# Where operand tiles stand modulo 256 bytes: moved low weights and activation tiles in a float32 two-block transformer kernel

## The chip, the core and the metric

The kernel runs on one NeuronCore of a Trainium2 chip. The metric is the device time of one execution in microseconds (us). TensorE does matrix products from SBUF into PSUM; VectorE, ScalarE and GpSimd do the rest; 16 DMA engines bring data from HBM. SBUF has 128 partitions, and an address in this text is a byte offset within a partition.

## What is computed

Two transformer blocks of width 2048 on 256 tokens, batch 1, all in float32. Both blocks are norm, projection, attention, projection, residual, norm, gated MLP (5632 wide), residual; the second has 16 more tokens in front (272 in all) and a convolution over three positions in its gate branch. Cut to the products with large weights:

```python
# first block                                       # weights
h = rms_norm(x, g) * (1 + scale_a) + shift_a
proj = h @ w_in                                     # 2048 x 5456
mixed = concat([diff_out, dsa_out]) @ w_o           # 2048 x 2048
h = rms_norm(x, g) * (1 + scale_f) + shift_f
ff = (silu(h @ w_gate) * (h @ w_up)) @ w_down       # 2048 x 5632 (twice), 5632 x 2048
# second block: w_in_2 2048 x 3904, w_q_up, w_kv_up, w_out_2, and
gc = conv_b + sum(conv_w[i] * shifted(h @ w_gate_2, i))
y = (silu(gc) * (h @ w_up_2)) @ w_down_2
```

`mod = silu(c) @ w_ada + b_ada` (2048 x 12288) gives shifts, scales and gates of the first block.

## The kernel before, in words

Activations are kept transposed: tile k of `x_hi` and `x_lo` holds features 128k to 128k + 127 on the partitions and the tokens along the free side. A float32 product is made from three faster ones (type float32r). Each operand is split into a high part (rounded to that type) and a low part (what is left), and the kernel adds high x high, low x high and high x low. The three are lines 2115, 2116 and 2117 in `dense` (line 2077). The stationary operand is a 128 x 128 piece of a weight buffer, the moving operand an activation tile of 256, 258 or 272 columns.

Weights come in units of 4 x 128 rows by 512 columns (1 MB, four buffers `raw`), in one order for the whole program. For each unit ScalarE writes `w_hi` (line 932) and VectorE `w_lo = raw - w_hi` (line 1462). There are two slots of each, `w_hi0`, `w_hi1`, `w_lo0`, `w_lo1` of 8192 bytes, used in turn. TensorE then does 4 output blocks (m) x 4 tiles (k) x 3 = 48 matmuls on the unit. A product over 2048 features has four units (`K16`), over 5632 features twelve (`K44`, the last four with three tiles).

In order of time: first projection (44 units, part by part: all columns for tiles 0 to 3, then for 4 to 7, and so on; 4 of the 44 have three output blocks), attention, `out1` with `w_o`, gate and up of the first block (11 pairs of `mlp1`), down (`hid_hi`, `hid_lo` as moving tiles), then the second block: its projection with 272 columns, two latent projections (272 columns, 8 short calls), `out2` with 258 columns, gate with 258 and up with 256 columns, and `down2` (lines 2796 to 2798), which has the hidden tiles as the stationary operand and 512 columns of weights as the moving one.

The places are made by `place` (line 236), which puts one tensor behind the other from byte 2208 on, rounded up to 32. `raw`, `w_hi` and `w_lo` have 8192 bytes each, `x_res`, `x_hi` and `x_lo` are 16 tiles of 272 float32 (17408 bytes = 68 x 256; one tile 1088 = 4 x 256 + 64), `hid_hi` and `hid_lo` 44 tiles of 256 float32 (45056 = 176 x 256; one tile 1024). Two gaps of 64 bytes stand between `x_hi` and `x_lo` and between `hid_hi` and `hid_lo`. So, counted from byte 2208 and modulo 256, all weight buffers are at 0, tile k of `x_hi` at 64k, of `x_lo` at 64k + 64, all tiles of `hid_hi` at 64, of `hid_lo` at 128.

Of the kernel before, what the change touches and what calls it, by code (L numbers as in the profile page):

```python
# [22 lines left out]
F32R = mybir.dt.float32r  # L23
# [4 lines left out]
P = 128  # L28
D = 2048
KT = D // P  # L30
S = 256
# [5 lines left out]
COLS = 512  # L37
UK = 4
RAW = 4
SPLIT = 2  # L40
# [115 lines left out]
def in1_width(n):  # L156

    return PROJ1 - 10 * COLS if ORDER_IN1[n] == 10 else COLS
# [69 lines left out]
def program(nc, a):  # L228
    with ExitStack() as ctx:
# [1 line left out]
            return ctx.enter_context(nc.semaphore(name))  # L231


        cursor = [2208]

        def place(name, shape, dt=F32, at=None):
            size = 4 * int(np.prod(shape[1:]))
            if at is None:
                at, cursor[0] = cursor[0], (cursor[0] + size + 31) // 32 * 32
            return nc.alloc_sbuf_tensor_at(name, shape, dt, offset=at)  # L240
# [8 lines left out]

        raw = [place(f"raw{i}", [P, UK * COLS]) for i in range(RAW)]  # L250
        w_hi = [place(f"w_hi{i}", [P, UK * COLS], F32R) for i in range(SPLIT)]
        w_lo = [place(f"w_lo{i}", [P, UK * COLS], F32R) for i in range(SPLIT)]
        x_res = place("x_res", [P, KT, N2])
        x_hi_at = cursor[0]
        x_hi = place("x_hi", [P, KT, N2], F32R)
        cursor[0] += 64
        x_lo_at = cursor[0]
        x_lo = place("x_lo", [P, KT, N2], F32R)
        branch_f = place("branch_f", [P, KT, S], at=x_hi_at)
        xmeta = place("xmeta", [META, D], at=x_lo_at)  # L260
        arena = cursor[0]
        hid_hi = place("hid_hi", [P, FT, S], F32R)
        cursor[0] += 64
        hid_lo = place("hid_lo", [P, FT, S], F32R)
        arena_end = cursor[0]
        cst = place("cst", [P, C_WIDTH])
# [11 lines left out]
        gain = place("gain", [P, 2, KT])  # L278
# [141 lines left out]
        norms, at = {}, dict(sq=0, col=0, presum=0, norm=0, group=0, use=0, split=0)  # L420
# [21 lines left out]
        def one(rows=P):  # L442
# [8 lines left out]
        kpe = proj2[0:64, T2_KPE, :]  # L451
        kpg = proj2[0:64, T2_CQ, :]
        norm("attn_pre", S, D, [[x_res[:, t, 0:S] for t in range(KT)]],
             [(0, x_res[:, t, 0:S], gain[:, 0, t:t + 1], x_hi[:, t, 0:S], x_lo[:, t, 0:S],
               mod[:, SH_A + t:SH_A + t + 1]) for t in range(KT)], True, given=x_sum)
        norm("diff", S, P, [[dout[:, h, :]] for h in range(8)],
             [(h, dout[:, h, :], lamv[:, 7:8], x_hi[:, h, 0:S], x_lo[:, h, 0:S], None) for h in range(8)], True)
# [1 line left out]
             [(0, branch_a[:, t, :], gain[:, 1, t:t + 1], branch_a[:, t, :]) for t in range(KT)], False,  # L459
             branch_a_ssq, direct=4)  # L460
        norm("ffn_pre", S, D, [[x_res[:, t, 0:S] for t in range(KT)]],
             [(0, x_res[:, t, 0:S], gain[:, 0, t:t + 1], x_hi[:, t, 0:S], x_lo[:, t, 0:S],
               mod[:, SH_F + t:SH_F + t + 1]) for t in range(KT)], True, column=True)
        norm("ffn_post", S, D, [[branch_f[:, t, :] for t in range(KT)]],
             [(0, branch_f[:, t, :], gain[:, 1, t:t + 1], branch_f[:, t, :]) for t in range(KT)], False,
# [122 lines left out]
        K16 = [(4 * q, 4) for q in range(4)]  # L588
        K_O = K16[2:] + K16[:2]
        K44 = [(4 * q, 4) for q in range(8)] + [(32 + 3 * q, 3) for q in range(4)]  # L590
        FOUR = [P] * 4
# [1484 lines left out]
        def _(pe):  # L2076
# [11 lines left out]
            def dense(units, rows, hi, lo, n, cols=None, width=COLS, step=1, last_unit=True, base=0, ready=None,  # L2088
# [38 lines left out]
                else:  # L2127
                    t.at += 4

            def xs(n):  # L2130
                return (lambda k: x_hi[:, k, 0:n]), (lambda k: x_lo[:, k, 0:n])

# [196 lines left out]
            for u in range(44):  # L2329
                part, n = divmod(u, 11)  # L2330
                if u == 0:
                    pe.wait_ge(tile_done, 4)
                    pe.wait_ge(bank_freed, 4)
                if n == 0 and part:
                    pe.wait_ge(n_lo, norms["attn_pre"]["first"]["split"] + 4 * part + 4)
                if n in (0, 2, 4, 6):
                    ada_quarter(ADA_IN1 + 2 * part, n // 2)
                ur.at = in1_unit(part, n)
                dense([K16[part]], TAIL1 if in1_width(n) < COLS else FOUR, *xs(S), S, width=in1_width(n),
                      banks=lambda m: in1_bank(u, m), lag=IN1_BANKS,  # L2340
                      tile_ready=None if u else "attn_pre")
                if n == 6:
                    ada_columns(ADA_IN1 + 2 * part)
                if n == 7:
                    s = ADA_IN1 + 2 * part + 1
                    pe.wait_ge(beside_used, 4 * part + 4)
                    pe.wait_ge(ada_copied, s)
                    for j in range(4):
                        ins = pe.matmul(bank[7][:, j:j + 1], acc_beside[:, P * j:P * j + P], one(), start=True,
                                        stop=True)  # L2350
                    ins.then_inc(ada_cols, 1)
                if part == 3 and n in (5, 7, 8, 10):
                    rotate_rows({5: 0, 7: 1, 8: 2, 10: 3}[n])
                if u == 23:
                    pe.wait_ge(vec_in, 16 * VEC_LOADS)
                    for j in range(3):
                        ins = pe.transpose(bank[6][:, P * j:P * j + P], packs[:, 1 + j, :], ident)
                    ins.then_inc(packs_turned, 1)
# [235 lines left out]
            spread("ffn_pre")  # L2594

            def mlp1(i, tile_ready=None, ada_block=None):
                dense(K16, FOUR, *xs(S), S, tile_ready=tile_ready,
                      step=2 if ada_block is not None else (lambda j: 9 if j == 0 else 1) if tile_ready else 1)
                if ada_block is not None:
                    pe.wait_ge(up_freed, up.value(4))  # L2600
                    ada_sum(ada_block, bank[7])
                dense(K16, FOUR, *xs(S), S, base=4, bank7=None if ada_block is None else ada_block + 1)
            mlp1(0, "ffn_pre")
            loop(4, (8, 4, 12, 4), lambda i: mlp1(i + 1, ada_block=i + ADA_MLP1))
            loop(6, (8, 4, 8, 4), lambda i: mlp1(i + 5))
# [227 lines left out]
```

## Time and profile before

| | |
|---|---|
| median of 3 runs | 2582.85 us (2581.18 to 2584.17) |
| profiled execution, its own time | 2583.03 us |
| its span in the trace | 2581.2 us |
| TensorE busy | 2475.4 us, 96% |
| VectorE, ScalarE, GpSimd busy | 1439.2, 1032.2, 292.0 us |
| mean granted clock of TensorE | 0.979 |
| read from HBM | 498.04 MB, 194 GB/s over the span |

The trace has every instruction's start and duration. Matmuls are pipelined: one that starts while another still runs is normal, and the pace is the time from one start to the next. The granted clock is 1.00 where TensorE runs at 2.4 GHz and 0.50 where it runs at 1.2 GHz.

### The profile page before, as it was taken

The numbers are of one execution on the slowest core, as the hardware profiler recorded it, in microseconds if no ns is written. First come the engines' busy times: TensorE is split into PE (matmuls) and PEld (weight loads), VectorE is DVE, ScalarE is ACT, GpSimd is POOL, SyncE is SP. The second block draws the span as 40 slices with busy tenths as digits, with TensorE's granted clock in tenths as the row PEclk, the third lists the DMA queues.
The fourth block names the chain that finished last, engine by engine and source line by source line (L and its number), as shares of the span: only waits on it lengthen the run. The fifth ranks groups of instructions, "written<-read, shape, count | busy, mean of one in ns | idle before, by whom it ended". The sixth has DMA issues, their size and how long they took to land.

```text
span 2581.2 us, 45664 instructions
## 1 busy us (share of the span) xinstructions
PE 2475.4 (96%) x18966; PEld 2296.1 (89%) x18966; DVE 1439.2 (56%) x1918; ACT 1032.2 (40%) x1332; POOL 292.0 (11%) x372
## 2 busy tenths in 40 slices
PE   6999988989999999999989998999999999999999
PEld 4999847979999999999979997778899999998877
DVE  3687657966674444444455555655655555554443
ACT  3533244344434343333334335443444444443332
POOL 5000122410100000011113002103000000000000
PEclk8999989989999999999989999999999999999999
DMA  9887864977786555555554451324455555554553
GB/s 353 290 288 268 286 211 168 337 271 237 249 294 200 184 185 189 178 185 186 179 146 149 139 160 54 126 71 131 132 188 185 179 179 179 180 185 169 193 202 131
DMA packets 263858, 504.18 MB, mean 195 GB/s; under 512 B 17152, under 2 KB 26283, under 8 KB 263467
## 3 DMA queue, kind: packets, MB, share of 16 engines
q1 hardware_dynamic: 257899, 494.97, 57.3%
q10 hardware_dynamic: 5840, 7.52, 0.9%
q8 instruction: 87, 1.43, 0.2%
q14 instruction: 32, 0.26, 0.0%
HBM read 498.04 MB, written 2.10 MB: 194 GB/s over the span
## 4 chain that ended last, share of the span: by engine, by line
PE 78%; DVE 8%; ACT 4%; issue 4%; DMA 3%; SPq 1%; ACTq 1%; POOL 1%; DVEq 0%; POOLq 0%
PE bank L2115 21%; PE bank L2117 20%; PE bank L2116 20%; ACT w_hi L932 3%; DVE w_lo L1462 3%; PE bank L2798 3%; PE bank L2796 3%; PE bank L2797 3%; PE bank L2150 1%; DMA raw<-in_w_in 1%; DVE ada_acc L1490 1%; DVE tmp L1596 1%; SPq L643 1%; PE bank L2259 1%; DMA staged<-in_w_ada 1%
## 5 line engine op out<-in xcount | busy, mean ns | idle before, releaser
L1462 DVE TENSOR_TENSOR w_lo<-raw,w_hi 128x2048 fp32r<-128x2048 f32 (+3 forms) x386 | 862.7, 2235 | 937.6 <-ACT w_hi L932 937.3
L2115 PE MATMUL bank<-x_hi,w_hi 128*128 128x256 f32 (+2 forms) x4608 | 1316.6, 286 | 37.1 <-DVE w_lo L1462 20.3
L2117 PE MATMUL bank<-x_hi,w_lo 128*128 128x256 f32 (+2 forms) x4608 | 1306.4, 283 | 0.0
L2116 PE MATMUL bank<-x_lo,w_hi 128*128 128x256 f32 (+2 forms) x4608 | 1300.7, 282 | 0.0
L932 ACT ACTIVATE w_hi<-raw 128x2048 fp32r<-128x2048 f32 (+3 forms) x386 | 718.7, 1862 | 1027.7 <-PE bank L2117 745.3
L2115 PEld LDWEIGHTS bank<-x_hi,w_hi 128*128 128x128 f32 x4608 | 872.2, 189 | 74.7 <-issue 41.3
L2116 PEld LDWEIGHTS bank<-x_lo,w_hi 128*128 128x128 f32 x4608 | 872.0, 189 | 1.2 <-issue 1.2
L2117 PEld LDWEIGHTS bank<-x_hi,w_lo 128*128 128x128 f32 x4608 | 871.8, 189 | 0.0
L2117 PE MATMUL bank<-hid_hi,w_lo 128*128 128x256 f32 x704 | 198.5, 282 | 0.0
L2115 PE MATMUL bank<-hid_hi,w_hi 128*128 128x256 f32 x704 | 196.8, 280 | 0.9 <-DVE w_lo L1462 0.9
L2116 PE MATMUL bank<-hid_lo,w_hi 128*128 128x256 f32 x704 | 197.1, 280 | 0.0
L797 POOL TENSOR_TENSOR hid_lo<-gpad,hid_hi 128x256 f32 x88 | 61.0, 726 | 996.4 <-ACT hid_hi L1417 503.2
L2796 PE MATMUL bank<-w_hi,hid_hi 128*128 128x512 f32 x352 | 138.4, 393 | 2.1 <-DVE gpad L2057 1.4
L2798 PE MATMUL bank<-w_lo,hid_hi 128*128 128x512 f32 x352 | 140.0, 398 | 0.0
L2797 PE MATMUL bank<-w_hi,hid_lo 128*128 128x512 f32 x352 | 138.0, 392 | 0.0
L2115 PEld LDWEIGHTS bank<-hid_hi,w_hi 128*128 128x128 f32 x704 | 133.7, 190 | 1.5 <-issue 1.5
L2116 PEld LDWEIGHTS bank<-hid_lo,w_hi 128*128 128x128 f32 x704 | 132.2, 188 | 0.0
L2117 PEld LDWEIGHTS bank<-hid_hi,w_lo 128*128 128x128 f32 x704 | 131.7, 187 | 0.0
L1490 DVE SCALAR_TENSOR_TENSOR ada_acc<-raw,csilu,ada_acc 128x512 f32<-128x512 f32 x120 | 97.2, 810 | 3.8 <-DMA raw<-in_w_ada 0.4
L2796 PEld LDWEIGHTS bank<-w_hi,hid_hi 128*128 128x128 f32 x352 | 66.2, 188 | 17.7 <-DVE w_lo L1462 2.0
L2797 PEld LDWEIGHTS bank<-w_hi,hid_lo 128*128 128x128 f32 x352 | 66.2, 188 | 16.2
L2798 PEld LDWEIGHTS bank<-w_lo,hid_hi 128*128 128x128 f32 x352 | 66.1, 188 | 14.3
(337 smaller groups left out, 1662.0 us busy)
## 6 DMA issues: line engine op xcount, KB each, us to landing
raw<-in_w_gate SPq DMA_DIRECT2D x88, 1024.0 KB, 5.2
raw<-in_w_up SPq DMA_DIRECT2D x88, 1024.0 KB, 5.2
raw<-in_w_ada SPq DMA_DIRECT2D x72, 1024.0 KB, 6.5
raw<-in_w_in SPq DMA_DIRECT2D x68, 1024.0 KB, 5.5
raw<-in_w_down SPq DMA_DIRECT2D x64, 1024.0 KB, 5.0
raw<-in_w_down SPq DMA_DIRECT2D x32, 768.0 KB, 4.3
beside<-in_w_ada SPq DMA_DIRECT2D x16, 1024.0 KB, 7.7
raw<-in_w_o SPq DMA_DIRECT2D x16, 1024.0 KB, 6.5
```

The lines of the kernel that those rows point to most:

```text
L643: sp.dma_start(staged[4 * s + q][:, :].rearrange("p (k c) -> p k c", k=nk), src).then_inc(staged_in[4 * s + q], 16)
L797: pool.tensor_tensor(lo, gpad[:, m, 0:S], hi, ALU.subtract).then_inc(hid_low, 1)
L932: act.activation(w_hi[ps][:, 0:width], raw[slot][:, 0:width], ACT.Copy).then_inc(hi_ready, 1)
L1462: dve.tensor_tensor(w_lo[ps][:, 0:width], raw[slot][:, 0:width], w_hi[ps][:, 0:width], ALU.subtract).then_inc(raw_free[slot], 1)
L1490: ins = dve.scalar_tensor_tensor(ada_acc[:, :], w, s, ada_acc[:, :], ALU.mult, ALU.add)
L1596: dve.scalar_tensor_tensor(dst, src, gcol, spread_row(name, g, rows, n["n"]), ALU.mult, ALU.mult).then_inc(n_app, 1)
L2115: pe.matmul(out, wh[:, k, c], hi(k0 + k), start=a0, stop=False)
L2116: pe.matmul(out, wh[:, k, c], lo(k0 + k), start=False, stop=False)
L2117: ins = pe.matmul(out, wl_[:, k, c], hi(k0 + k), start=False, stop=z)
L2796: pe.matmul(out, hi, wh[:, k, :], start=j == 0 and k == 0, stop=False)
L2797: pe.matmul(out, lo, wh[:, k, :], start=False, stop=False)
L2798: ins = pe.matmul(out, hi, wl_[:, k, :], start=False, stop=j == 11 and k == nk - 1)
```

## The change

It moves operands in SBUF and changes nothing else: no instruction, wait, transfer or order.

- `w_lo1` is put first, then 128 bytes are left free, then `w_lo0`, then 96 bytes. So `w_lo0` stands at 128, `w_lo1` at 0, and what follows starts at 224.
- The two gaps of 64 bytes go. `x_hi`, `x_lo` then start at 224 both (tile k at 224 + 64k), `hid_hi` and `hid_lo` at 224.
- A new function `spaced` lays tiles of 256 columns over the room of `x_hi` and `x_lo`, 1024 bytes apart with 256 bytes more after each four, so that the tiles of one unit of weights have one place: `xin` for the first projection at 48, 80, 96, 112 for the four units (high and low alike), `xff` for gate and up of the first block at 192 (high) and 192, 192, 224, 224 (low). The norms ahead of these stages write there, and `dense` reads there.
- `out1` and the second block go on using `x_hi` and `x_lo`.

```diff
-        cursor = [2208]
+        first = 2208
+        cursor = [first]
...
-        w_lo = [place(f"w_lo{i}", [P, UK * COLS], F32R) for i in range(SPLIT)]
+        w_lo1 = place("w_lo1", [P, UK * COLS], F32R)
+        cursor[0] += 128
+        w_lo = [place("w_lo0", [P, UK * COLS], F32R), w_lo1]
+        cursor[0] += 96
         x_res = place("x_res", [P, KT, N2])
         x_hi_at = cursor[0]
         x_hi = place("x_hi", [P, KT, N2], F32R)
-        cursor[0] += 64
         x_lo_at = cursor[0]
         x_lo = place("x_lo", [P, KT, N2], F32R)
+
+        def spaced(name, phases):
+
+            tiles = []
+            for part, start in enumerate((x_hi_at, x_lo_at)):
+                tiles.append([])
+                for k in range(KT):
+                    at_ = 4 * S * k + 256 * (k // 4) + (phases[k // 4][part] - (start - first)) % 256
+                    room = place(f"{name}{part}_{k}", [P, S + 8], F32R, at=start + at_ // 32 * 32)
+                    tiles[part].append(room[:, at_ % 32 // 4:at_ % 32 // 4 + S])
+            return tiles
+        xin_hi, xin_lo = spaced("xin", [(48, 48), (80, 80), (96, 96), (112, 112)])
+        xff_hi, xff_lo = spaced("xff", [(192, 192), (192, 192), (192, 224), (192, 224)])
...
         hid_hi = place("hid_hi", [P, FT, S], F32R)
-        cursor[0] += 64
         hid_lo = place("hid_lo", [P, FT, S], F32R)
...
-             [(0, x_res[:, t, 0:S], gain[:, 0, t:t + 1], x_hi[:, t, 0:S], x_lo[:, t, 0:S],
+             [(0, x_res[:, t, 0:S], gain[:, 0, t:t + 1], xin_hi[t], xin_lo[t],
...
-             [(0, x_res[:, t, 0:S], gain[:, 0, t:t + 1], x_hi[:, t, 0:S], x_lo[:, t, 0:S],
+             [(0, x_res[:, t, 0:S], gain[:, 0, t:t + 1], xff_hi[t], xff_lo[t],
...
-                dense([K16[part]], TAIL1 if in1_width(n) < COLS else FOUR, *xs(S), S, width=in1_width(n),
+                dense([K16[part]], TAIL1 if in1_width(n) < COLS else FOUR, *tiles(xin_hi, xin_lo), S, width=in1_width(n),
...
-                dense(K16, FOUR, *xs(S), S, tile_ready=tile_ready,
+                dense(K16, FOUR, *tiles(xff_hi, xff_lo), S, tile_ready=tile_ready,
...
-                dense(K16, FOUR, *xs(S), S, base=4, bank7=None if ada_block is None else ada_block + 1)
+                dense(K16, FOUR, *tiles(xff_hi, xff_lo), S, base=4, bank7=None if ada_block is None else ada_block + 1)
```

## Rows read from the trace of the kernel before

**Rows 1.** The page: busy time, chain that ended last, the two split instructions.
```profile
PE 2475.4 (96%) x18966; PEld 2296.1 (89%) x18966; DVE 1439.2 (56%) x1918; ACT 1032.2 (40%) x1332; POOL 292.0 (11%) x372
...
PE 78%; DVE 8%; ACT 4%; issue 4%; DMA 3%; SPq 1%; ACTq 1%; POOL 1%; DVEq 0%; POOLq 0%
...
L1462 DVE TENSOR_TENSOR w_lo<-raw,w_hi 128x2048 fp32r<-128x2048 f32 (+3 forms) x386 | 862.7, 2235 | 937.6 <-ACT w_hi L932 937.3
...
L932 ACT ACTIVATE w_hi<-raw 128x2048 fp32r<-128x2048 f32 (+3 forms) x386 | 718.7, 1862 | 1027.7 <-PE bank L2117 745.3
```

**Rows 2.** Stages: window, its us, busy us (instructions) by engine, granted clock, DMA share, GB/s.
```profile
43.00:323.00 280.00, 274.94 (x2258) 257.72 (x2259) 203.42 (x278) 107.32 (x119) 26.55 (x25) 0.99 0.82 287
...
556.00:1067.50 511.50, 504.65 (x4256) 500.42 (x4257) 278.32 (x225) 206.47 (x194) 29.50 (x41) 1.00 0.64 212
1067.50:1319.50 252.00, 251.09 (x2133) 250.35 (x2133) 103.20 (x51) 92.62 (x73) 29.53 (x29) 1.00 0.51 172
1342.00:1556.00 214.00, 211.03 (x1612) 197.17 (x1612) 122.81 (x165) 85.75 (x109) 22.73 (x23) 0.99 0.51 161
...
1812.00:2329.00 517.00, 509.99 (x4226) 505.51 (x4227) 288.56 (x338) 222.57 (x281) 27.16 (x42) 1.00 0.56 178
2331.00:2577.00 246.00, 245.30 (x1076) 198.81 (x1075) 103.29 (x54) 85.20 (x54) 0.00 (x0) 1.00 0.51 173
```

**Rows 3.** TensorE in order of time (start, us): first and 193rd, gate and up.
```profile
999.84 0.28 PE L2115 MATMUL bank<-x_hi,w_hi 128*128 128x256 f32 x1
...
1022.24 0.28 PE L2115 MATMUL bank<-x_hi,w_hi 128*128 128x256 f32 x1
```

**Rows 4.** In order of time: first and 193rd, last up block of the first block.
```profile
1044.95 0.28 PE L2115 MATMUL bank<-x_hi,w_hi 128*128 128x256 f32 x1
...
1067.57 0.28 PE L2115 MATMUL bank<-hid_hi,w_hi 128*128 128x256 f32 x1
```

**Rows 5.** In order of time: first and 190th, down projection of the first block.
```profile
1195.88 0.28 PE L2115 MATMUL bank<-hid_hi,w_hi 128*128 128x256 f32 x1
...
1218.14 0.28 PE L2115 MATMUL bank<-hid_hi,w_hi 128*128 128x256 f32 x1
```

**Rows 6.** In order of time: first and 37th, first projection.
```profile
235.95 0.28 PE L2115 MATMUL bank<-x_hi,w_hi 128*128 128x256 f32 x1
...
240.15 0.28 PE L2115 MATMUL bank<-x_hi,w_hi 128*128 128x256 f32 x1
```

**Rows 7.** In order of time: second block, 132 matmuls of gate, then 192 of up.
```profile
2195.81 0.28 PE L2115 MATMUL bank<-x_hi,w_hi 128*128 128x258 f32 x1
...
2211.65 0.28 PE L2115 MATMUL bank<-x_hi,w_hi 128*128 128x256 f32 x1
...
2234.26 0.28 PE L2115 MATMUL bank<-x_hi,w_hi 128*128 128x258 f32 x1
```

**Rows 8.** In order of time: 272 columns, 47 matmuls; then 11 with 64 weight columns.
```profile
1441.61 0.29 PE L2115 MATMUL bank<-x_hi,w_hi 128*128 128x272 f32 x1
...
1447.49 0.28 PE L2117 MATMUL bank<-x_hi,w_lo 128*128 128x272 f32 x1
...
1488.47 0.29 PE L2115 MATMUL bank<-x_hi,w_hi 128*64 128x272 f32 x1
...
1489.84 0.28 PE L2117 MATMUL bank<-x_hi,w_lo 128*64 128x272 f32 x1
```

**Rows 9.** 272 columns at the lower clock: first and tenth; their stretch as in rows 2.
```profile
1600.94 0.43 PE L2115 MATMUL bank<-x_hi,w_hi 128*64 128x272 f32 x1
...
1602.98 0.43 PE L2115 MATMUL bank<-x_hi,w_hi 128*64 128x272 f32 x1
...
1600.72:1602.98 2.26, 2.26 (x12) 2.24 (x11) 0.47 (x1) 2.26 (x5) 0.00 (x0) 0.52 0.00 0
```

**Rows 10.** In order of time: first and 115th, second down projection, 512 columns.
```profile
2427.64 0.39 PE L2796 MATMUL bank<-w_hi,hid_hi 128*128 128x512 f32 x1
...
2453.99 0.39 PE L2796 MATMUL bank<-w_hi,hid_hi 128*128 128x512 f32 x1
```

More of the change, by code:

```diff
@@ L2128, in dense, with tiles @@
                     t.at += 4
+            def tiles(hi, lo):
+                return (lambda k: hi[k]), (lambda k: lo[k])
             def xs(n):
```

## The prediction

> **What bounds the kernel now.** I read the page of the profile first, then the busy time by stage, then single matmuls in order of time. TensorE is busy for 2475.4 us of a span of 2581.2 us, and it carries 78% of the chain that ended last [rows 1]. The stages show where: in the gate and up projections of the first block it is busy 504.65 of 511.50 us, in the first down projection 251.09 of 252.00, in the first projection 274.94 of 280.00, and the second block looks alike [rows 2]. So in all dense stages the end is set by how fast TensorE starts one matmul after the other, and nearly every nanosecond per matmul is a nanosecond of the kernel.
>
> The busy time of a matmul (0.28 us) says nothing on that, since matmuls overlap; the reader has to take starts. In the gate and up stage 192 matmuls of 128x256 start between 999.84 and 1022.24 us: 22.40 / 192 = 116.7 ns each, and no wait lies between [rows 3]. The granted clock there is 1.00, the upper level of 2.4 GHz [rows 2], at which 256 columns take 106.7 ns. So each matmul costs 10.0 ns more than its columns. That this is not a fixed price of an instruction is shown by the one place where the same stream runs at the lower level: from 1600.94 to 1602.98 us, at a granted clock of 0.52 over the window, nine matmuls of 272 columns take 2.04 us, 226.7 ns each, which is 272 columns at 1.2 GHz with nothing on top [rows 9]; at the upper level 47 matmuls of 272 columns take 5.88 us, 125.1 ns each, 11.8 ns over their columns [rows 8]. Something is short only at full speed, and the operands' reads are the candidate that this change touches.
>
> **What the trace says of addresses.** Take all places from the first tile, modulo 256 bytes, as the diff does. Now every weight buffer stands at 0, and rows of weights are multiples of 512 bytes. The tiles x_hi and x_lo are 1088 bytes long, so tile k stands at 64k, its low part at 64k + 64: four different pairs in turn. The hidden tiles are 1024 bytes long, so all stand at 64 (high) and 128 (low). Three findings:
> 1. Every steady pace is a multiple of 6.67 ns for the shortest repeat. I call three matmuls (high x high, low x high, high x low, one k) a triple. Down: 189 matmuls in 22.26 us, 353.3 ns a triple = 53 x 6.67 [rows 5]. Gate and up: 350.0 a triple, and the repeat is four triples, 1400 = 210 x 6.67 [rows 3]. With 258 columns: 132 matmuls in 15.84 us, 360.0 = 54 x 6.67 [rows 7]. With 512 columns: 114 in 26.35 us, 693.4 = 104 x 6.67 [rows 10]. This is an estimate of mine from these rows; it says that a tile arrangement that repeats at each triple can gain or lose only in steps of about 6.7 ns.
> 2. The same lines, the same form and the same addresses have two paces. The last up block of the first block starts 192 matmuls in 22.62 us, 117.8 ns each [rows 4], against 116.7 before [rows 3], and the up block of the second block 192 in 22.61 us [rows 7]. The pace also hangs on how the stream was entered. The difference is 3.3 ns a triple.
> 3. With half the weight columns (64) the pace of 272 columns is 1.37 us / 11 = 124.5 ns against 125.1 [rows 8]. So the weights' own reads carry little of the 10 ns, and moving w_lo alone should do little.
>
> **The change, part by part.** No instruction is added or taken away and no wait moves; only addresses. (a) w_lo of slot 0 goes to 128, of slot 1 stays at 0. (b) First projection: tiles now 1024 bytes apart, high and low both at 48, 80, 96, 112 for the four parts. (c) Gate and up of the first block: 192 for both, low at 224 from tile 8. (d) Down: both at 224. (e) Not named in the title, but done: the two gaps of 64 bytes go, so in out1 and in all of the second block x_hi and x_lo stand at the same 224 + 64k, and the second down's stationary tiles at 224.
>
> The counts follow from the loops: first projection 688 triples, gate and up 22 x 64 = 1408, down 4 x 4 x 44 = 704, together 2800. Untargeted: out1 256, second block 2256 (gate and up 1408, in2 496, out2 256, the two latent projections 96), second down 352, together 2864.
>
> Prices. Down repeats at each triple before and after, so it can only step; it is the slowest arrangement of 256 columns that the trace has. I take one step down, 353.3 to 346.7: 704 x 6.67 = 4.7 us. Gate and up come from 350.0, and within one unit of weights all tiles will now have one pair of places, so it too repeats at each triple and must go to 346.7 or up to 353.3. I take 346.7, 3.33 x 1408 = 4.7 us. The first projection has 36 matmuls in 4.20 us, 350.0 a triple [rows 6], so by the same step 3.33 x 688 = 2.3 us. Why down and not up: the room above the columns' time is 10.0 ns a matmul, 30 a triple, so there are about four steps below and the nearest arrangement with constant places (down) is the one that stands highest. For the untargeted 2864 triples no row has equal places for high and low, so I bound them by the spread that one arrangement shows, 3.33 ns a triple to either side [rows 3, 4], plus or minus 9.5 us, and take zero, since no row speaks for a side. (a) is taken at zero by finding 3, within the same bound.
>
> Sum: 4.7 + 4.7 + 2.3 = 11.7 us. The profiled execution took 2583.0 us (span 2581.2), the median of three is 2582.85, so 2583.0 - 11.7 = 2571.3.
>
> **Cover.** A unit of weights is 48 matmuls, 5.60 us. ScalarE's 1.86 and VectorE's 2.24 us for it [rows 1] make 4.1 us, and with 5.55 us per unit that stays hidden; only where VectorE also empties banks is some of it lost, well under 1 us in all. Next late would be the transfers in the first projection: 287 GB/s at a DMA share of 0.82, against 0.64 in gate and up [rows 2]. If the first projection were held by these, its 2.3 us are lost.
>
> **Rules against the trace.** The trace has one form with paces of 116.7 and 117.8 ns and a constant-place arrangement at 117.8 [rows 3 to 5]. The Trainium skill (SBUF — State Buffer, Who interferes with whom) says that TensorE has two independent read ports, one for the moving operand and one for weights, and never waits for anyone; by it places in memory cost nothing and the change gives 0. It also gives (TensorE: Matmul & The Clock Gate, "Wait — 56ns, not 53.3ns?") columns at 2.4 GHz plus about 2.5 ns from start to start, which is 109.2 ns for 256 columns; the trace has 116.7, so it does not agree for these operands. If the whole difference of 7.5 ns went in the 8400 targeted matmuls the time would be 2520, and I don't hold that for likely.
>
> **The rivals.**
> *Second step.* The places were apt enough for two steps, 340.0 ns a triple. Another 2800 x 6.67 = 18.7 us: 2552.6. For it: the 30 ns of room. Against it: all the arrangements of 256 columns in the rows lie within 3.3 ns a triple of each other.
> *Nothing.* The 10 ns are a fixed toll at full speed, and places only shuffle it among neighbours: 2583. For it: weights of 64 and 128 columns hardly differ, and four pairs of places and one pair come within 1% of each other. Against it: the constant-place stage is the slower one in every unit. The skill's rule of independent ports, above, is the same case.
> *Equal places collide.* High and low tile at the same place is new, and it holds in the first projection, in half of gate and up, in down and in all untargeted triples: 688 + 704 + 704 + 2864 = 4960. At the price of the slower pace, 3.33 ns a triple, that is 16.5 us: 2599.5. Set against the targeted gain it decides from about 3500 triples on (11.7 us / 3.33). For it: now the low tile always stands 64 behind the high one, and nothing shows what 0 does. Against it: the high and the low tile are never moving at the same time, they follow each other, and in down a high tile already follows a high one at the same place.
>
> **Numbers.** Forecast (one step in the targeted stages) 0.43, second step 0.15, nothing 0.17, equal places collide 0.25. Faster by over 0.2% (5.2 us, about what a measurement of this kernel can tell from no change) is the first two, 0.58; within it 0.17; slower 0.25. The sides are of both signs, so the forecast's own range, from the bound of the untargeted triples, is 2562 to 2581; the whole range goes from below the second step, 2545, to the collision's price, 2600.
>
> **What would show it.** In the changed kernel's trace: down at 115.6 ns from start to start (three matmuls in 346.7) and gate and up at the same pace for all k in a unit; 113.3 for the second step; 117.8 for none. In the second block, matmuls of 258 columns at 120.0, of 272 at 125, three of 512 at 693, if it is untouched; 116.7 to 118 instead of 117.8 for its 256 columns. I am wrong if the targeted stages keep their pace, if their pace is no multiple of 6.67 a triple, or if the second block's pace moves by more than 1.1 ns a matmul: it has more triples than the targeted part and could outweigh it.

## The result and the profile after

The changed kernel takes 2586.57 us (median of 18), the kernel before in the same runs 2581.53 us: a ratio of 1.0017, 95% interval 1.001 to 1.0024. It is slower by 5 us. One of the 18 executions took 8412.31 us; the ratio leaves it out, and the median of the other 17 is 2586.50. The profiled execution took 2591.96 us, 5 us over the median, so the times below that rest on one trace are paces, which do not depend on how long single waits are.

The page of the changed kernel: against [rows 1] TensorE's busy time has grown by 10.7 us, and that of the other engines has moved by 1.2 us at most.

```profile
span 2590.2 us, 45664 instructions
...
PE 2486.1 (96%) x18966; PEld 2304.7 (89%) x18966; DVE 1439.3 (56%) x1918; ACT 1033.4 (40%) x1332; POOL 291.2 (11%) x372
...
PE 78%; DVE 8%; ACT 5%; issue 4%; DMA 3%; SPq 1%; ACTq 1%; POOL 1%; DVEq 0%; POOLq 0%
...
L1477 DVE TENSOR_TENSOR w_lo<-raw,w_hi 128x2048 fp32r<-128x2048 f32 (+3 forms) x386 | 863.1, 2236 | 942.1 <-ACT w_hi L947 941.8
L947 ACT ACTIVATE w_hi<-raw 128x2048 fp32r<-128x2048 f32 (+3 forms) x386 | 719.3, 1864 | 1029.0 <-PE bank L2132 757.8
```

Single matmuls of the changed kernel in order of time (start, us), gate and up of the first block. The first pair encloses 84 matmuls with both tiles at 192, the second 36 with 192 and 224 and w_lo at 128 (slot 0), the third 36 with 192 and 224 and w_lo at 0 (slot 1):

```profile
1006.73 0.28 PE L2130 MATMUL bank<-xff,w_hi 128*128 128x256 f32 x1
1016.25 0.28 PE L2130 MATMUL bank<-xff,w_hi 128*128 128x256 f32 x1
...
1017.66 0.28 PE L2130 MATMUL bank<-xff,w_hi 128*128 128x256 f32 x1
1021.90 0.28 PE L2130 MATMUL bank<-xff,w_hi 128*128 128x256 f32 x1
...
1023.32 0.28 PE L2130 MATMUL bank<-xff,w_hi 128*128 128x256 f32 x1
1027.60 0.28 PE L2130 MATMUL bank<-xff,w_hi 128*128 128x256 f32 x1
```

9.52 / 84 = 113.3 ns, 4.24 / 36 = 117.8, 4.28 / 36 = 118.9; per triple (three matmuls of one k) 340.0, 353.3 and 356.7. Before, this stage ran at 350.0 [rows 3] or 353.3 [rows 4]. Half of the stage has come to the 340.0 that the prediction called the second step; the other half has lost.

Down (288 matmuls, answers to [rows 5]), the first projection's third part at 96 (24, to [rows 6]), and in the second block up (192) and gate (96, to [rows 7]) and the second down (177, to [rows 10]):

```profile
1148.30 0.28 PE L2130 MATMUL bank<-hid_hi,w_hi 128*128 128x256 f32 x1
1182.38 0.28 PE L2130 MATMUL bank<-hid_hi,w_hi 128*128 128x256 f32 x1
...
188.22 0.28 PE L2130 MATMUL bank<-xin,w_hi 128*128 128x256 f32 x1
191.10 0.28 PE L2130 MATMUL bank<-xin,w_hi 128*128 128x256 f32 x1
...
2079.31 0.29 PE L2130 MATMUL bank<-x_hi,w_hi 128*128 128x256 f32 x1
2102.05 0.28 PE L2130 MATMUL bank<-x_hi,w_hi 128*128 128x258 f32 x1
2114.20 0.29 PE L2130 MATMUL bank<-x_hi,w_hi 128*128 128x258 f32 x1
2125.78 0.29 PE L2130 MATMUL bank<-x_hi,w_hi 128*128 128x256 f32 x1
...
2407.16 0.40 PE L2815 MATMUL bank<-w_hi,hid_hi 128*128 128x512 f32 x1
2448.29 0.39 PE L2815 MATMUL bank<-w_hi,hid_hi 128*128 128x512 f32 x1
```

A triple is 34.08 / 96 = 355.0 in down (353.3 before), 2.88 / 8 = 360.0 at 96 (350.0), 22.74 / 64 = 355.3 in up (353.3), 11.58 / 32 = 361.9 in gate (360.0), 41.13 / 59 = 697.1 in the second down (693.4). Everything but the tiles at 192 is slower.

For whole stages I take the mean over all starts of a stage that follow each other at less than 160 ns (512 columns: 280 ns), which leaves out the waits, times three. Times the triples of the stage this is what the pace is worth:

| stage (triples) | ns a triple before | after | us | forecast us |
|---|---|---|---|---|
| first projection (688) | 352.0 | 355.4 | +2.4 | -2.3 |
| gate and up, first block (1408) | 350.7 | 348.6 | -2.9 | -4.7 |
| down, first block (704) | 353.3 | 354.9 | +1.1 | -4.7 |
| out1 (256) | 351.1 | 355.7 | +1.2 | 0 |
| second block to out2 (848) | 370.8 | 371.4 | +0.5 | 0 |
| gate, second block (704) | 360.1 | 361.3 | +0.8 | 0 |
| up, second block (704) | 353.3 | 355.3 | +1.5 | 0 |
| second down (352) | 693.4 | 698.4 | +1.7 | 0 |
| sum | | | +6.3 | -11.7 |

The sum of +6.3 stands beside the measured +5.0: the pace of TensorE is enough to account for the loss.

### The profile page after: what moved, and what is told of

Its sections match the earlier page's. It is cut to its first block, busy times and chain, and to the rows that moved or that the text cites. A ratio compares the mean times of both kernels' runs of the same rounds, so it can differ in the third digit from the quotient of the medians.

```text
span 2590.2 us, 45664 instructions
## 1 busy us (share of the span) xinstructions
PE 2486.1 (96%) x18966; PEld 2304.7 (89%) x18966; DVE 1439.3 (56%) x1918; ACT 1033.4 (40%) x1332; POOL 291.2 (11%) x372
## 4 chain that ended last, share of the span: by engine, by line
PE 78%; DVE 8%; ACT 5%; issue 4%; DMA 3%; SPq 1%; ACTq 1%; POOL 1%; DVEq 0%; POOLq 0%
PE bank L2130 21%; PE bank L2132 20%; PE bank L2131 20%; ACT w_hi L947 3%; DVE w_lo L1477 3%; PE bank L2815 3%; PE bank L2817 3%; PE bank L2816 3%; DMA raw<-in_w_in 2%; PE bank L2169 1%; SPq L658 1%; DVE tmp L1611 1%; DVE ada_acc L1505 1%; PE bank L2278 1%; DMA raw<-in_w_gate 1%
## 5 line engine op out<-in xcount | busy, mean ns | idle before, releaser
L2130 PE MATMUL bank<-x_hi,w_hi 128*128 128x256 f32 (+2 forms) x2512 | 727.7, 290 | 19.5 <-DVE w_lo L1477 9.1
L2131 PE MATMUL bank<-x_lo,w_hi 128*128 128x256 f32 (+2 forms) x2512 | 717.2, 286 | 0.0
L2132 PE MATMUL bank<-x_hi,w_lo 128*128 128x256 f32 (+2 forms) x2512 | 716.8, 285 | 0.0
L2130 PEld LDWEIGHTS bank<-x_hi,w_hi 128*128 128x128 f32 x2512 | 477.7, 190 | 34.9 <-issue 21.8
L2131 PEld LDWEIGHTS bank<-x_lo,w_hi 128*128 128x128 f32 x2512 | 478.6, 191 | 0.7 <-issue 0.7
L2132 PEld LDWEIGHTS bank<-x_hi,w_lo 128*128 128x128 f32 x2512 | 478.4, 190 | 0.0
L2130 PE MATMUL bank<-xff,w_hi 128*128 128x256 f32 x1408 | 397.0, 282 | 8.9 <-DVE w_lo L1477 4.8
L2131 PE MATMUL bank<-xff,w_hi 128*128 128x256 f32 x1408 | 393.8, 280 | 0.0
L2132 PE MATMUL bank<-xff,w_lo 128*128 128x256 f32 x1408 | 392.5, 279 | 0.0
L2130 PEld LDWEIGHTS bank<-xff,w_hi 128*128 128x128 f32 x1408 | 265.3, 188 | 13.7 <-DVE w_lo L1477 7.2
L2131 PEld LDWEIGHTS bank<-xff,w_hi 128*128 128x128 f32 x1408 | 266.2, 189 | 0.0
L2130 PE MATMUL bank<-xin,w_hi 128*128 128x256 f32 (+1 forms) x688 | 199.4, 290 | 5.9 <-DVE w_lo L1477 4.5
L2131 PE MATMUL bank<-xin,w_hi 128*128 128x256 f32 (+1 forms) x688 | 195.4, 284 | 0.0
L2130 PEld LDWEIGHTS bank<-xin,w_hi 128*128 128x128 f32 (+1 forms) x688 | 131.3, 191 | 21.9 <-issue 15.1
```

The source lines that it names most:

```text
L2130: pe.matmul(out, wh[:, k, c], hi(k0 + k), start=a0, stop=False)
L2131: pe.matmul(out, wh[:, k, c], lo(k0 + k), start=False, stop=False)
L2132: ins = pe.matmul(out, wl_[:, k, c], hi(k0 + k), start=False, stop=z)
```

## The experiments

Paces below are made in the same way. "Slot 0" and "slot 1" say which weight slot the unit used. The diffs are against the changed kernel if nothing else is said.

### One part undone or done alone

**w_lo_back.**

```diff
-        w_lo1 = place("w_lo1", [P, UK * COLS], F32R)
-        cursor[0] += 128
-        w_lo = [place("w_lo0", [P, UK * COLS], F32R), w_lo1]
-        cursor[0] += 96
+        w_lo = [place(f"w_lo{i}", [P, UK * COLS], F32R) for i in range(SPLIT)]
+        cursor[0] += 224
```

> The changed kernel with both low-weight slots at 0 again; every tile keeps its new place. In the changed kernel three matmuls of one k (a triple) take 342.0 and 342.6 ns in gate and up where high and low tile are both at 192, and 353.5 and 356.1 where the low one is at 224; in the first projection's last part (112, 112) 345.0 in slot 1 (w_lo at 0) but 354.8 in slot 0 (w_lo at 128). Theory P (the pair of moving tiles sets the pace, w_lo does not): all these stay, and the time stays within 3 us of the changed kernel. Theory W (w_lo at 128 disturbs where the pair is not robust): slot 0 of (112, 112) falls from 354.8 to 345 or 340, the hidden tiles and the second block lose their extra 1 to 2 ns a triple, and the time falls by 3 to 8 us.

Measured: 2589.74 us, 1.0028 of before (1.0018 to 1.0039). Neither theory held. Slot 0 of (112, 112) did fall, from 354.8 to 343.1. But gate and up rose from 348.6 to 353.3, and most at 192, where I expected nothing: 342.0 and 342.6 became 352.7 and 347.8. Down stayed at 355.0. The trace of w_lo_back shows 72 matmuls there (both tiles at 192) in 8.48 us, 117.8 ns each:

```profile
1006.21 0.28 PE L2128 MATMUL bank<-xff,w_hi 128*128 128x256 f32 x1
1014.69 0.28 PE L2128 MATMUL bank<-xff,w_hi 128*128 128x256 f32 x1
```

So w_lo at 128 is worth something, but not by making a pace faster; see all_192.

**ff_192.**

```diff
-        xff_hi, xff_lo = spaced("xff", [(192, 192), (192, 192), (192, 224), (192, 224)])
+        xff_hi, xff_lo = spaced("xff", [(192, 192), (192, 192), (192, 192), (192, 192)])
```

> The changed kernel with the low tiles of gate and up at 192 for all sixteen k, not 224 from k = 8 on. Theory P: units 3 and 4 of each product go from 353.5 and 356.1 ns a triple to 342 like units 1 and 2, 704 triples x 12.7 ns = 9 us, so about 2577.5 us. Rival: the 342 comes from the half of the product that stands first (its distance to the weights, the entry from a wait), not from equal places; then nothing moves, 2586.

Measured: 2575.77 us, 0.9978 (0.9968 to 0.9989). All four units went to 340.1 to 340.7 ns a triple: the rival falls, and this kernel is faster than both. 300 matmuls without a break, over all four units, take 34.00 us, 113.3 ns each:

```profile
979.10 0.28 PE L2130 MATMUL bank<-xff,w_hi 128*128 128x256 f32 x1
1013.10 0.28 PE L2130 MATMUL bank<-xff,w_hi 128*128 128x256 f32 x1
```

**w_lo_alone.** Against the kernel before:

```diff
-        w_lo = [place(f"w_lo{i}", [P, UK * COLS], F32R) for i in range(SPLIT)]
+        w_lo1 = place("w_lo1", [P, UK * COLS], F32R)
+        gain_at = cursor[0]
+        gain = place("gain", [P, 2, KT])
+        w_lo = [place("w_lo0", [P, UK * COLS], F32R), w_lo1]
+        mod = place("mod", [P, 96])
```

> The kernel before with only w_lo of slot 0 at 128; small tensors fill the holes, so that all tiles keep their old places modulo 256. Theory P: all paces as in the kernel before (350.7 ns a triple in gate and up, 353.3 down, 360 and 353.3 in the second block), 2581.5 us within 2. Theory W: slot 0 alone gets slower in every stage, by 1 to 4 ns a triple, 2 to 10 us in all.

Measured: 2583.64 us, 1.001 (0.9999 to 1.0021), so not told from no change. The paces moved by up to 2.2 ns a triple to both sides: gate and up 352.3 (+1.6), second projection 377.3 (+1.8), up of the second block 351.9 (-1.4), second down 691.2 (-2.2), worth +3.2 us in all.

**targets_only.** Holes filled as above, so that `x_hi` is at 0, and the two gaps are back:

```diff
+        cursor[0] += 64
         x_lo_at = cursor[0]
...
+        cursor[0] += 64
         hid_lo = place("hid_lo", [P, FT, S], F32R)
```

> The changed kernel's new tiles for the first projection and gate and up, and w_lo of slot 0 at 128, but the plain tiles of out1 and the second block at 0 and 64 plus 64k and the hidden tiles at 64 and 128, as in the kernel before. If the untargeted move (high and low at the same 224 plus 64k, hidden at 224) costs what the stages of the two traces say (out1 and second projection 1.2 us, down 1.0, gate and up of the second block 1.4, second down 1.6), the time is 5 us less than the changed kernel's, 2581.5. Rival: it costs nothing and the first projection is all of the loss: 2586.

Measured: 2581.26 us, 1.0005 (0.9996 to 1.0015), as expected to 0.3 us: the places that this run takes back cost the 5 us that the stages said. They are the untargeted ones and the hidden tiles of the first down (354.9 to 354.4 ns a triple, 0.4 us of it). Without them the change brings nothing either, since the first projection (355.3) loses what gate and up (348.4) gain.

### All targeted tiles at 192

**all_192.** w_lo at 0 in both slots, `x_hi` at 0, and

```diff
+        cursor[0] += 64
         x_lo_at = cursor[0]
...
-        xin_hi, xin_lo = spaced("xin", [(48, 48), (80, 80), (96, 96), (112, 112)])
-        xff_hi, xff_lo = spaced("xff", [(192, 192), (192, 192), (192, 224), (192, 224)])
+        xin_hi, xin_lo = spaced("xin", [(192, 192)] * 4)
+        xff_hi, xff_lo = spaced("xff", [(192, 192)] * 4)
...
+        cursor[0] += 128
         arena = cursor[0]
```

> Low weights at 0, the plain tiles of out1 and the second block as in the kernel before (0 and 64 plus 64k), and 192 for high and low in the first projection, in gate and up and in down. Theory P: these 2800 triples all go to 340 to 342 ns: 688 x 10 + 1408 x 9 + 704 x 12 ns = 28 us less than the kernel before, some 2554 us, with the second block unchanged. Theory W or the first-half rival: no stage but half of gate and up reaches 342, and the time stays above 2570.

Measured: 2562.53 us, 0.9932 (0.9916 to 0.9949): faster by 20 us, not 28. The second block's paces stayed but for its second down, which has the hidden tiles as the stationary operand (693.4 to 687.0 for a triple of 512 columns, 2.3 us); gate and up is at 344.2, down at 346.7, the first projection at 343.3. These are not paces but mixtures of two. In the trace of all_192, same lines, same places, 168 matmuls in 19.79 us (117.8 ns), and after a break 72 in 8.16 us (113.3 ns):

```profile
628.31 0.28 PE L2129 MATMUL bank<-xff,w_hi 128*128 128x256 f32 x1
648.10 0.28 PE L2129 MATMUL bank<-xff,w_hi 128*128 128x256 f32 x1
656.31 0.28 PE L2129 MATMUL bank<-xff,w_hi 128*128 128x256 f32 x1
664.47 0.28 PE L2129 MATMUL bank<-xff,w_hi 128*128 128x256 f32 x1
```

A row of 12 matmuls (one output block of a unit) without a wait takes 1360 ns or 1413 ns, hardly anything else: 221 and 93 of 317 in gate and up, 62 and 61 of 123 in down. In these two stages no stretch without a wait has rows of both paces: the pace changes where the stream was broken by a wait, and then lasts until the next break. What in a break decides for one or the other, no run tells.

**all_192_w128.** The same with w_lo of slot 0 at 128, by the diff of w_lo_alone.

> As all_192, but w_lo of slot 0 at 128 again (small tensors fill the holes, all other places stay). In all_192 three matmuls of a k take either 340.0 or 353.3 ns with the same places, and the pace changes only after a break in the stream (219 of the 317 whole rows of gate and up at 340.0, about half of down). With w_lo at 128 in ff_192 gate and up was at 340.0 nearly throughout. Theory C (capture): w_lo at 128 does not change the fast pace but makes the slow one unstable, so all 2800 triples go to 340 to 341: about 3.7 x 1408 + 6.7 x 704 + 2 x 688 ns = 11 us less than all_192, some 2551 us. Rival: the entry decides by luck of the breaks' lengths, then a mix stays and the time is 2558 to 2565.

Measured: 2556.54 us, 0.9906 (0.989 to 0.9923). Slow rows: 15 of 316 in gate and up, 3 of 123 in down; paces 341.0 and 340.5. The intervals of the two ratios overlap; the traces tell them apart. All 18 slow rows are in slot 1, three in each of six units that were entered after a wait, and there the pace does change without a wait: in each of the six it turns fast when the next unit begins, whose w_lo is at 128. The first pair below encloses 36 matmuls in slot 1 (4.24 us, 117.8 ns), the second 36 of the next unit in slot 0 (4.08 us, 113.3 ns); no start between them comes later than 120 ns after the one before.

```profile
795.64 0.28 PE L2130 MATMUL bank<-xff,w_hi 128*128 128x256 f32 x1
799.88 0.28 PE L2130 MATMUL bank<-xff,w_hi 128*128 128x256 f32 x1
801.26 0.28 PE L2130 MATMUL bank<-xff,w_hi 128*128 128x256 f32 x1
805.34 0.28 PE L2130 MATMUL bank<-xff,w_hi 128*128 128x256 f32 x1
```

**w_lo_both_128.** Against all_192_w128, both slots of w_lo at 128:

```diff
-        w_lo1 = place("w_lo1", [P, UK * COLS], F32R)
         gain_at = cursor[0]
         gain = place("gain", [P, 2, KT])
-        w_lo = [place("w_lo0", [P, UK * COLS], F32R), w_lo1]
+        w_lo = [place(f"w_lo{i}", [P, UK * COLS], F32R) for i in range(SPLIT)]
```

> all_192_w128 with w_lo of both slots at 128. With w_lo at 0 in both slots 93 of 317 whole rows (four triples) of gate and up ran at the slow pace of 353.3 ns, with slot 0 at 128 only 15, and those begin in slot 1. Theory C (at 128 the slow pace cannot last): none or nearly none is left, the targeted stages are at 340.0 to 340.5 ns a triple, and the first projection and gate and up gain 1 us or less. Rival: 128 in both slots is as bad as 0 in both, what helps is that the slots differ: then a mix of the two paces comes back, 60 or more of 317.

Measured: 2554.87 us, 0.9898 (0.9882 to 0.9915). Slow rows (1413 ns): 1 of 315, 0 of 123, and 0 of 109 in the first projection, where six rows of the narrow units take 1400 to 1434 (see weights_64). Gate and up is at 340.5, down at 340.1, the first projection at 342.2. The rival falls: it is the place 128, not the difference of the slots. The gain over all_192_w128 is within the noise. Gate and up, then down, in all_192 and in w_lo_both_128 (window, its us, busy us by engine, granted clock, DMA share, GB/s): the same work in 3.3 and 4.4 us less.

```profile
549.60:1052.60 503.00, 496.00 (x4256) 491.74 (x4257) 277.96 (x224) 206.75 (x193) 29.30 (x41) 1.00 0.63 216
1052.70:1299.90 247.20, 245.97 (x2129) 245.25 (x2128) 102.58 (x50) 92.55 (x72) 29.83 (x29) 1.00 0.51 175
```

```profile
545.60:1045.30 499.70, 491.39 (x4255) 486.99 (x4256) 278.39 (x224) 206.24 (x193) 29.28 (x40) 0.99 0.65 218
1045.40:1288.20 242.80, 241.35 (x2129) 240.65 (x2129) 102.77 (x51) 92.82 (x72) 29.94 (x29) 1.00 0.53 178
```

**out1_192.** Against all_192_w128; the norm of the differential heads and the sparse heads write to `xin` too:

```diff
-                dense(K_O, FOUR, *xs(S), S, step=2, ready=ready, bank_ready=bank_ready)
+                dense(K_O, FOUR, *tiles(xin_hi, xin_lo), S, step=2, ready=ready, bank_ready=bank_ready)
```

> all_192_w128 with the tiles of out1 at 192 too (high and low, 1024 bytes apart). If the place alone decides, out1's 256 triples go from 352.2 to 341 ns, 2.9 us less, some 2553.5 us. Rival: out1 waits for VectorE's splits (its busy share is highest there), then its stage keeps its 106 us and the time stays at 2556.5.

Measured: 2554.73 us, 0.9897 (0.9881 to 0.9914). out1 went from 352.2 to 343.6 ns a triple and its stage from 106.7 to 104.3 us. In time it is not told from all_192_w128, but its stage is. This and w_lo_both_128 are the fastest kernels of the study, 1% below the kernel before.

### Where the good place is

**map_equal, map_pairs, map_fine.** `xin` and `xff` give each group of four tiles its own pair of places, so that one run measures six pairs. Against all_192_w128 (the plain tiles and the hidden tiles stand elsewhere too: in map_equal `x_lo` at 64k and both hidden tiles at 128, in map_pairs `x_lo` at 128 + 64k and `hid_lo` at 224):

```diff
# map_equal
+ spaced("xin", [(0, 0), (64, 64), (128, 128), (160, 160)])
+ spaced("xff", [(208, 208), (208, 208), (176, 176), (176, 176)])
# map_pairs
+ spaced("xin", [(192, 0), (192, 64), (192, 128), (0, 192)])
+ spaced("xff", [(128, 192), (128, 192), (192, 160), (192, 160)])
# map_fine
+ spaced("xin", [(184, 184), (188, 188), (196, 196), (200, 200)])
+ spaced("xff", [(112, 112), (112, 112), (144, 144), (144, 144)])
```

> A map of equal places for high and low tile, w_lo at 128 in slot 0 and at 0 in slot 1. First projection: 0, 64, 128, 160; gate and up: 208 in the first half, 176 in the second; down: 128; second block: 0 plus 64k for both. Known so far, ns a triple: 48: 355, 80: 357, 96: 360, 112: 344, 192: 340, 224: 355. Theory N (192 is the middle of a narrow good place): 208 and 176 are near 340, 0, 64 and 128 at 353 or more. Rival R (repeats every 64 or 80 bytes, since 112 and 192 are both good): 0, 64 or 128 is at 340 too.

> A map of unequal places (high, low), w_lo at 128 in slot 0 and at 0 in slot 1. First projection: (192, 0), (192, 64), (192, 128), (0, 192); gate and up: (128, 192) in the first half, (192, 160) in the second; down (192, 224); second block 64k for high, 128 + 64k for low. Theory E (equality is what counts, at a good place): all of them at 350 or more. Rival H (the high tile's place counts, it moves in two of three matmuls): the ones with high at 192 are nearer to 340 than (0, 192) and (128, 192).

> A fine map of equal places for high and low, w_lo at 128 in slot 0 and at 0 in slot 1. First projection: 184, 188, 196, 200; gate and up: 112 in the first half, 144 in the second; down stays at 192. Measured so far, ns a triple: 176: 354 to 358, 192: 340, 208: 356. If the good place is one 16-byte line, 196 and 200 stay at 340 to 345 and 184 and 188 are at 353 or more; if it is the start at exactly 192, all four are at 353 or more; if it is a smooth dip, 188 and 196 lie between. For 112: about 340 in slot 1 and 355 in slot 0, as in the changed kernel's first projection; 144 is open.

Each map is one execution: 2592.84 us (map_equal), 2591.30 (map_pairs), 2571.25 (map_fine). Measured, ns a triple in slot 0 (w_lo at 128) and slot 1 (at 0), high and low tile at the same place; 48 to 112 and 224 are from the changed kernel, 192 is gate and up of all_192_w128. One place in two stages can differ by 2 ns (128 in slot 1: 356.5 in the first projection, 358.5 in down of map_equal):

| place | slot 0 | slot 1 | | place | slot 0 | slot 1 |
|---|---|---|---|---|---|---|
| 0 | 356.6 | 359.6 | | 176 | 353.8 | 357.6 |
| 48 | 354.4 | 355.0 | | 184 | 360.0 | 359.7 |
| 64 | 356.5 | 353.4 | | 188 | 352.5 | 354.4 |
| 80 | 356.1 | 358.0 | | **192** | 340.3 | 341.7 |
| 96 | 360.5 | 359.9 | | 196 | 362.6 | 365.4 |
| 112 | 354.8 | 345.0 | | 200 | 363.9 | 361.0 |
| 128 | 355.4 | 356.5 | | 208 | 356.7 | 355.7 |
| 144 | 355.2 | 356.6 | | 224 | 355.0 | 354.9 |
| 160 | 354.3 | 353.9 | | | | |

Unequal pairs are at 353 to 362: (192, 0) 354.5 and 354.3, (192, 64) 362.4 and 353.4, (192, 128) 357.4 and 356.4, (0, 192) 353.1 and 353.8, (128, 192) 359.7 and 360.7, (192, 160) 353.3 and 353.4. So both tiles have to be there (theory E), and the good place is not a region but exactly 192: one float32 further on, at 196, is among the worst (362.6 and 365.4), and one float32 before, at 188, is as slow as most places (352.5 and 354.4). 112 is the second, and only with w_lo at 0; its mean of 345.0 is 340.0 once the stream has settled, as in gate and up of map_fine in slot 1, 36 matmuls in 4.08 us:

```profile
1005.79 0.28 PE L2130 MATMUL bank<-xff,w_hi 128*128 128x256 f32 x1
1009.87 0.28 PE L2130 MATMUL bank<-xff,w_hi 128*128 128x256 f32 x1
```

The two maps also show what the untargeted move did. The second block's up has tiles that step by 64 bytes with k. With high and low tile at unequal places, 64 bytes apart (targets_only) or 128 (map_pairs), it is at 351.9 ns a triple; with both at the same place, from 0 (map_equal) or from 224 (the changed kernel), at 355.5 and 355.3. out1 goes the same way: 352.5 and 352.3 against 356.7 and 355.7. So for tiles of 256 columns that step with k, equal places cost 3 to 4 ns a triple, and where they start hardly counts. In gate (258 columns) it is about 1 ns, and with 272 columns there is no clear difference. Of the 192 matmuls of one up block, map_pairs takes 22.52 us and map_equal 22.75:

```profile
2128.20 0.28 PE L2131 MATMUL bank<-x_hi,w_hi 128*128 128x256 f32 x1
2150.72 0.28 PE L2131 MATMUL bank<-x_hi,w_hi 128*128 128x258 f32 x1
```

```profile
2128.53 0.28 PE L2129 MATMUL bank<-x_hi,w_hi 128*128 128x256 f32 x1
2151.28 0.28 PE L2129 MATMUL bank<-x_hi,w_hi 128*128 128x258 f32 x1
```

**weights_64.** Against all_192_w128, everything from `w_hi` on is moved by 64 bytes:

```diff
+        cursor[0] += 64
         w_hi = [place(f"w_hi{i}", [P, UK * COLS], F32R) for i in range(SPLIT)]
...
+        xin_hi, xin_lo = spaced("xin", [(192, 192), (0, 0), (176, 176), (112, 112)])
+        xff_hi, xff_lo = spaced("xff", [(0, 0), (0, 0), (192, 192), (192, 192)])
```

> All weight buffers moved on by 64 bytes (w_hi at 64, w_lo of slot 0 at 192 and of slot 1 at 64). First projection: equal places 192, 0, 176, 112; gate and up: 0 in the first half, 192 in the second; down at 0. Theory D (the distance from weights to moving tile counts, modulo 256, 192 - 0): the good place moves on to 0, so 0 gives 340 to 342 in all three stages, 192 gives 353 to 360, and 176 (= 112 + 64) is at 344 in slot 1. Rival S (the tile's own place counts, against something that does not move): 192 stays at 340 and 0 stays at 353 or more.

Measured (one execution, 2570.53 us): theory D in each point. With weights at 64, tiles at 0 are at 342.6 and 342.2 in gate and up and at 340.6 in down, tiles at 192 at 355.0 and 356.5, and 176 is at 354.2 in slot 0 and 342.7 in slot 1, as 112 was. From the trace, 84 matmuls with tiles at 0 in 9.52 us and 36 with tiles at 192 in 4.26 us, 113.3 and 118.3 ns:

```profile
999.68 0.28 PE L2131 MATMUL bank<-xff,w_hi 128*128 128x256 f32 x1
1009.20 0.29 PE L2131 MATMUL bank<-xff,w_hi 128*128 128x256 f32 x1
1010.62 0.29 PE L2131 MATMUL bank<-xff,w_hi 128*128 128x256 f32 x1
1014.88 0.29 PE L2131 MATMUL bank<-xff,w_hi 128*128 128x256 f32 x1
```

What counts is the distance from the weights to the moving tiles modulo 256 bytes: in ff_192 the tiles of the second and fourth unit stand 256 bytes further on, modulo 512, than those of the first and third, and all four units are fast; 64 and 192 differ (356.5 and 340.3 in slot 0). The narrow units of the first projection agree. Their rows of weights have 336 columns, 1344 bytes, so the weights themselves step by 64 with k and are at the distance of 192 for one k of four only (the prediction's "rows of weights are multiples of 512 bytes" leaves these four units out). In w_lo_both_128 their 128-column output block without a wait takes 1433 or 1434 ns for 12 matmuls, three times of three, with the same tiles at 192. The share of w_hi and w_lo in it was told apart only for w_lo: its slot 0 stands 128 further on, and at a distance of 192 from w_hi the fast pace holds with either.

## Why the prediction was wrong

**What bounds the kernel** held. The changes of pace come near the measured times: +6.3 against +5.0 us for the change, -21.9 against -19.8 for all_192, -0.1 against -0.1 for targets_only, -5.1 against -6.5 for ff_192 (paces of one trace against medians). In other runs they are further off: +11.2 against +7.4 for w_lo_back, -29.1 against -24.8 for all_192_w128, -32.2 against -26.1 for out1_192. In all_192_w128 a part of the pace is lost to waits: its first projection is 3.4 us shorter than before where the pace gives 5.9, its gate and up 11.4 where the pace gives 13.6.

**"it is the slowest arrangement of 256 columns that the trace has. I take one step down"** is the step that failed. I took that a tile at a constant place would gain because there was room below. The trace before had four pairs of places, at multiples of 64 and all with the low tile 64 behind; from them nothing follows for 48 or 224. Nor was down the slowest by its constant places: the second block's up, with the same stepping pairs as the first block's gate and up, takes 353.3 as well (192 matmuls in 22.61 us, [rows 7]), so the argument against the rival "nothing", that the constant-place stage is the slower one, did not hold either. Of the places that the change picks, one is good (192 for both, 704 triples), 112 is good in slot 1 once the stream has settled, and the rest are at 353 to 360, above the 350.7 that the stepping pairs had in gate and up. First projection: -2.3 forecast, +2.4 measured. Down: -4.7 forecast, +1.1.

**Gate and up**: the sign was right and the terms were not. Two steps (340.0) came in half of it, +3 to +6 ns in the other half, -2.9 us together against -4.7.

**"A tile arrangement that repeats at each triple can gain or lose only in steps of about 6.7 ns"** failed. Down after the change takes 355.0 a triple, 53.25 steps; in slot 0 its rows read 115 118 117 123 116 116 120 123 117 115 117 123 ns and repeat only after four triples (1420 ns = 213 x 6.67), in slot 1 after eight matmuls (947 ns = 142 x 6.67). A multiple of 6.67 ns still held for the whole repeat in these rows (and for the 1360 ns at 192 and the 1440 at 96), but constant places do not make the repeat one triple.

**"Moving w_lo alone should do little"**: held alone (w_lo_alone, not told from no change), wrong together. With the tiles at 192 the same move is worth 7 us in paces (all_192 to all_192_w128), since the slow one of the two paces does not outlast a unit of slot 1 there. (Finding 3's 124.5 ns comes from rounded starts; the trace has 124.9 against 125.1, so that the weights' columns carry even less. Their place is another matter.) I had seen the two paces (finding 2), and took them for a spread, not for something that a place can select.

**The untargeted triples** were taken at zero within 9.5 us. They cost 5.7 us by the table, and targets_only, which takes down back too, bears it out with 5. The cost was in the bound, not in the forecast. Of the 18 us between the forecast and the table, 12.3 are in the targeted stages and 5.7 here.

**The rivals.** "Nothing" (2583) came nearest in time, by gains and losses that cancel, not by its mechanism: ff_192 shows that places count. "Equal places collide" had the sign right, and its price for the tiles that step with k (3.4 to 3.6 ns a triple in the second block's up, 3.33 priced), but not its rule: equal places at 192 are the fastest of all, and unequal pairs with one tile at 192 are slow. "Second step" was real, at 192 and, in slot 1, at 112. The time of 2586.6 is inside the whole range and outside the forecast's own. By its size the loss lies within the 5.2 us that had 0.17; by the interval it is a loss, and that side had 0.25.

**The rules against the trace.** The Trainium skill (SBUF — State Buffer, Who interferes with whom) says that TensorE has two independent read ports and never waits for anyone. The runs disagree with what the prediction drew from it, that places cost nothing: the same matmul goes from 113.3 to 121.8 ns (365.4 / 3) by the distance of its two operands in memory. At the lower clock no effect of the place is seen: in the changed kernel's first projection, granted clock 0.50, 12 matmuls with tiles at 112 in slot 0 take 2.56 us, 213.3 ns each, which is 256 columns at 1.2 GHz. Tiles at 192 (all_192_w128) and at 184 (map_fine) start 213.3 ns apart too at the start of the first projection, where the clock is the lower one.

```profile
287.63 0.41 PE L2130 MATMUL bank<-xin,w_hi 128*128 128x256 f32 x1
290.19 0.41 PE L2130 MATMUL bank<-xin,w_hi 128*128 128x256 f32 x1
...
287.63:290.19 2.56, 2.56 (x14) 2.56 (x13) 1.74 (x1) 0.79 (x1) 2.45 (x2) 0.50 0.91 311
```

What inside the chip makes the distance count stays open; no run here looks at it.

## What to carry to other kernels

When TensorE streams without waits, measure start to start per matmul and compare it with the columns at the granted clock: what is over can hang on the bytes between the operands, and one run can map many places if each group of tiles gets its own. Do not take a place found for one arrangement over to its neighbours or to an unequal pair, and count what a changed layout does to the stages that were not meant: here these were half of the triples, and cost 5.7 us. A stream can have two lasting paces for the same addresses, so look at its pace after each break, not only at the mean.

## What the runs showed of the hardware that was not expected

- 128x256 float32r matmuls, each with a new 128x128 stationary operand, run at 113.3 ns if both moving tiles start exactly 192 bytes (modulo 256) behind the weights, and at 116.7 to 121.8 at nearly all other places that were tried (112 reaches 113.3 with the low weights at 0). 4 bytes further on, at 196, they take 120.9 and 121.8, 4 bytes before, at 188, 117.5 and 118.1.
- Moved together by 64 bytes, weights and tiles keep this: 113.3 ns at 0 with weights at 64.
- With w_hi and w_lo at 0 and the tiles at 192 there are two lasting paces, 113.3 and 117.8 ns, which in gate and up and in down change only at a break. With w_lo of one slot at 128 the slow one ends, without a break, where a unit of that slot begins. With w_lo at 128 in both slots the slow one is gone (1 row of 315).
- With tiles of 256 columns that step by 64 bytes with k, high and low at the same place cost 3.4 to 3.6 ns a triple against 64 or 128 bytes apart (second block's up).
- The stationary side counts too: in the second down, whose stationary tiles are the hidden ones, a triple of 512 columns takes 687.0 ns with them at 192 (all_192), 693.4 at 64 and 128, 699.8 at 224 (w_lo_back); the low weights are at 0 in all three.
